# One ring of five buffers for the raw weights and their low part, four buffers for the high part, and a split that runs three units ahead

## What is computed

```python
c_act = jax.nn.silu(c)
for i in range(DEPTH):                                  # 2 layers
    mod = c_act @ ada_w[i] + ada_b[i]                   # 1024 x 6144 each
    sh1, sc1, g1, sh2, sc2, g2 = jnp.split(mod[:, None, :], 6, axis=-1)
    h = rms_norm(x, norm_mix[i]) * (1.0 + sc1) + sh1
    if i % N_MIXERS == 0:
        y = dilated_attention(h, attn_w_qkv[a], attn_w_out[a], ...)   # w_qkv 1024 x 9216
    else:
        y = hgrn2_mixer(h, hgrn_w_in[a], hgrn_w_out[a], ...)          # w_in 1024 x 4096
    x = x + g1 * y
    h = rms_norm(x, norm_ffn[i]) * (1.0 + sc2) + sh2
    x = x + g2 * (jax.nn.silu(h @ w1) * (h @ w3)) @ w2                # 1024 x 2816, twice, and 2816 x 1024
```

## Time and profile before

| | |
|---|---|
| runs of the kernel before | 910.11 us median of 3 (909.47 to 910.36) |
| the profiled execution | span 910.1 us from the first to the last instruction; no other time lies around it in the run times |
| busy in it | PE 847.7 us, DVE 623.6 us, ACT 426.3 us, POOL 119.3 us |
| granted clock of PE | 0.980 of full speed over the span |
| DMA | 188.96 MB, 208 GB/s over the span |

### The profile page before, as it was taken

One profiled execution on the slowest core, in us unless ns is written; L12 is line 12 of the kernel. 1 busy time (PEld: TensorE's weight loads), 2 busy tenths in 40 slices (PEclk: granted clock), 3 DMA queues, 4 the chain that ended last, 5 costly groups with the idle time before them and its releaser, 6 DMA issues.

```text
span 910.1 us, 10752 instructions
## 1 busy us (share of the span) xinstructions
PE 847.7 (93%) x4195; PEld 709.3 (78%) x4195; DVE 623.6 (69%) x749; ACT 426.3 (47%) x515; POOL 119.3 (13%) x159
## 2 busy tenths in 40 slices
PE   1599999999999979999999979999989799999997
PEld 0477888889888858888888857888877588888886
DVE  5879678677686767766777775895774754454543
ACT  3255446545455355333433446658554553433431
POOL 4101001010010010111111100462620000000000
PEclk9999999999999999999999979999979899999999
DMA  9899766876767627889889835444224175555541
GB/s 339 284 271 310 240 224 214 274 222 231 230 221 243 190 89 249 286 277 316 283 278 318 294 109 182 139 139 139 93 93 139 46 225 191 185 185 185 185 139 46
DMA packets 119607, 188.96 MB, mean 208 GB/s; under 512 B 5580, under 2 KB 90758, under 8 KB 119558
## 3 DMA queue, kind: packets, MB, share of 16 engines
q1 hardware_dynamic: 105350, 137.90, 47.4%
q0 software_dynamic: 14208, 50.39, 15.9%
HBM read 187.18 MB, written 1.09 MB: 207 GB/s over the span
## 4 chain that ended last, share of the span: by engine, by line
PE 81%; DVE 8%; DMA 4%; ACT 3%; issue 2%; SPq 2%; DVEq 0%; ACTq 0%
PE bank L390 69%; PE bank L659 2%; PE bank L508 2%; PE bank L484 2%; DMA raw<-in_attn_w_qkv_dram 1%; DVE wlo L1052 1%; PE bank L469 1%; PE bank L604 1%; ACT arena L774 1%; PE bank L434 1%; SPq L268 1%; PE bank L406 1%; DMA arena<-in_distance_table_dram 1%; DMA bias_rows<-arena 1%; DMA ada_w<-in_ada_w_dram 1%
## 5 line engine op out<-in xcount | busy, mean ns | idle before, releaser
L1052 DVE TENSOR_TENSOR wlo<-raw,whi 128x2048 fp32r<-128x2048 f32 x126 | 288.7, 2291 | 126.6 <-ACT whi L724 126.3
L390 PE MATMUL bank<-whi,hT_hi 128*128 128x512 f32 (+1 forms) x800 | 315.7, 395 | 8.7 <-DVE hT_lo L1145 8.3
L724 ACT ACTIVATE whi<-raw 128x2048 fp32r<-128x2048 f32 x126 | 241.5, 1916 | 150.3 <-PE bank L390 120.5
L390 PE MATMUL bank<-whi,hT_lo 128*128 128x512 f32 (+1 forms) x800 | 308.5, 386 | 0.0
L390 PE MATMUL bank<-wlo,hT_hi 128*128 128x512 f32 (+1 forms) x800 | 308.0, 385 | 0.0
L390 PEld LDWEIGHTS bank<-whi,hT_hi 128*128 128x128 f32 x800 | 152.7, 191 | 42.6 <-DVE hT_lo L1145 10.1
L390 PEld LDWEIGHTS bank<-whi,hT_lo 128*128 128x128 f32 x800 | 152.4, 191 | 30.4
L390 PEld LDWEIGHTS bank<-wlo,hT_hi 128*128 128x128 f32 x800 | 152.8, 191 | 28.8 <-issue 1.0
L1077 DVE SCALAR_TENSOR_TENSOR acc<-ada_w,cact,acc 128x1024 f32<-128x1024 f32 x80 | 102.3, 1279 | 25.0 <-DMA ada_w<-in_ada_w_dram 24.6
L390 PE MATMUL bank<-whi,oT_hi 128*128 128x512 f32 x240 | 97.4, 406 | 3.6 <-DVE oT_lo L1430 1.6
L312 POOL DMA_DIRECT2D ada_w<-in_ada_w_dram x80 | 42.6, 532 | 408.3 <-DVE acc L1077 408.3
(11 more groups left out here) (137 smaller groups left out, 734.0 us busy)
## 6 DMA issues: line engine op xcount, KB each, us to landing
raw<-in_ffn_w_dram SPq DMA_DIRECT2D x88, 512.0 KB, 4.9
ada_w<-in_ada_w_dram POOLq DMA_DIRECT2D x80, 512.0 KB, 5.2
raw<-in_attn_w_qkv_dram SPq DMA_DIRECT2D x64, 512.0 KB, 4.8
raw<-in_ffn_w_dram SPq DMA_DIRECT2D x22, 1024.0 KB, 6.0
raw<-in_hgrn_w_in_dram SPq DMA_DIRECT2D x16, 1024.0 KB, 5.4
arena<-in_ada_w_dram POOLq DMA_DIRECT2D x16, 512.0 KB, 6.6
raw<-in_attn_w_qkv_dram SPq DMA_DIRECT2D x4, 1024.0 KB, 5.1
raw<-in_attn_w_out_dram SPq DMA_DIRECT2D x4, 1024.0 KB, 6.0
```

Source lines behind the costliest of these rows:

```text
L390: mm = nc.tensor.matmul(d[:, 0:n], l, r[:, k, cut], start=first and k == 0 and q == 0, stop=last and k == nk - 1 and q == 2)
L724: return nc.scalar.activation(dst, src, ACT.Copy)
L1052: nc.vector.tensor_tensor(wlo[:, m % SPL, :], raw[:, m % RAW, :], fp(whi[:, m % SPL, :]), ALU.subtract).then_inc(s["split"], 1)
```

## The change

`raw` and `wlo` become two views of one piece of memory with five buffers. The split of unit `m` now writes `raw - whi` over the raw weights of the same buffer, so the buffer is free for the next load when PE is through with the unit, and not when DVE has split it: the load of unit `m` waits for PE's unit `m-5` (`pe_unit`). `whi` gets four buffers in place of three; the rounding of unit `m` waits for PE's unit `m-4`. `AHEAD` is 3: beside PE's unit `m` stands round and split of unit `m + 3`, and unit 2 is rounded and split in front of the loop. Together the buffers take nine units of memory, as before, and 64 bytes.

```diff
-RAW = 3
-SPL = 3
-AHEAD = 2
+RAW = 5
+SPL = 4
+AHEAD = 3
...
-        raw = sb("raw", [P, RAW, UNIT])
+        ring_at = -(-nc.sbuf_base // 64) * 64
+        ring = sb("ring", [P, RAW * UNIT + 16])
+        raw = nc.alloc_sbuf_tensor_at("raw", [P, RAW, UNIT], F32, offset=ring_at)
+        wlo = nc.alloc_sbuf_tensor_at("wlo", [P, RAW, UNIT], F32R, offset=ring_at)
         whi = sb("whi", [P, SPL, UNIT], F32R)
-        wlo = sb("wlo", [P, SPL, UNIT], F32R)
...
                 if m >= RAW:
-                    sp.wait_ge(s["split"], m - RAW + 1)
+                    sp.wait_ge(s["pe_unit"], m - RAW + 1)
...
-                sl = m % SPL
-                w = [v[:, sl, :].rearrange("p (k n) -> p k n", k=nk) for v in (whi, wlo)]
+                w = [v.rearrange("p (k n) -> p k n", k=nk) for v in (whi[:, m % SPL, :], wlo[:, m % RAW, :])]
...
             norm_round(0, 1)
+            round_unit(2)
...
-                nc.vector.tensor_tensor(wlo[:, m % SPL, :], raw[:, m % RAW, :], fp(whi[:, m % SPL, :]), ALU.subtract
+                nc.vector.tensor_tensor(wlo[:, m % RAW, :], raw[:, m % RAW, :], fp(whi[:, m % SPL, :]), ALU.subtract
...
             norm_rest(0, 1)
+            split_unit(2)
```

## The result

| | before | changed |
|---|---|---|
| median | 909.47 us (907.99 to 910.36, 5 runs) | 918.28 us (913.22 to 920.66, 5 runs) |
| ratio | | 1.0089, 95% interval 1.0063 to 1.0115 |
| profiled execution, span | 910.1 us | 918.9 us |
| granted clock | 0.980 | 0.978 |

A forecast was written before the change was run, and what follows sets the result against it. PE, busy 93% of the span, was taken to bound the kernel, with DVE on the path at the start. 910.1 + 3.8 (start) + 2.6 (clock) + 0 (later loads) = 916.5 us; range 911.9 to 921.

The forecast's parts named there:

- signs of being wrong: Wrong if load 3 moved, PE waited ahead of L604, or boundaries changed length; units from 10 on should last as before.
- What bounds the kernel, nothing to gain from the depth: Whole kernel: PE busy 93% of the span; its waits for split units, all a deeper split could save, are 0.2 us.
- The start, 3.8 us: Before the first block's transposes: reordered DVE work ends the first normalisation later, bounds 3.4 to 4.3 us, taken as 3.8.
- two feared waits: At the start, DVE waiting for load 4 before split 4, and for the third `ada_op`'s DMA: 0 to 0.8 us each.
- The clock, 2.6 us: Behind PE's gap of 5.7 us at the start: half clock costs dense matmuls 1.7 to 4.1 us, taken as 2.6.
- The later loads, 0 us: First network: ACT waits for most of some 29 loads, roughly 40 us in all, but PE loses 0.
- the cover: Slack before PE's transposes in the first network: landings up to 9.0 us tolerated, some 0.3 us spare at the worst.
- Equal size, equal time for the matmuls: Whole kernel: rounding, split and matmuls as many as before and of the same size, so no cost in the sum.
- rival "faster": Second boundary, behind unit 72: freer DMA engines win up to 2.7 us, giving 907.4; chance 0.07 together with a trace rule.

The follow-up runs named there:

- E8: Changed kernel without the 64 bytes behind the ring, `AHEAD` back at 2 and unit 2 not prepared ahead of the loop: 908.18 us, 0.9996 of before.
- E7: Changed kernel without the 64 bytes, and with round and split behind the other work in the first three steps: 909.10 us, 1.0005 of before.
- E5: Changed kernel without the 64 bytes behind the ring: 914.05 us, 1.0065 of before.
- E3: Changed kernel with round and split behind the other work in the first three steps, 64 bytes kept: 914.00 us, 1.0059 of before.
- E4: Changed kernel with 20 matmuls of 512 columns put into PE's gap behind unit 3: 917.69 us, 1.0092 of before.
- E11: E5 with 20 matmuls put into PE's gap behind unit 3: 914.37 us, 1.0059 of before.
- E12: E7 with each load waiting for one more unit of PE, m-4 instead of m-5: 1019.66 us, 1.1219 of before.
- E6: Kernel before with 64 unused bytes between `whi` and `wlo`, nothing else: 922.58 us, 1.0160 of before.
- E9: Kernel before with the first block squared and normalised earlier and the first network's `ada_op` spread over 30 steps: 907.35 us, 0.9982 of before.
- E1: Kernel before with 64 unused bytes behind the raw ring: 908.32 us, 1.0003 of before.
- E2: Changed kernel with 128 instead of 64 unused bytes behind the ring: 921.45 us, 1.0142 of before.
- E10: E5 with the first block squared and normalised earlier and the first network's `ada_op` spread over 30 steps: 908.37 us, 0.9997 of before.

## Why the prediction was right

The number was right, and so was the mechanism of its two terms, the order at the start and the clock behind the gap. But the sum of the two was 6.4 us and 8.8 were measured; the missing part is the balance of things that the prediction had at nothing, and that they nearly cancelled is luck. Three of its own signs of being wrong came: load 3 is split 0.3 us later, the boundaries change length, and the units from 10 on are not as long as before.

*What bounds the kernel, nothing to gain from the depth.* Right, and shown by E8 and E7: neither ring nor depth moves the time by what can be measured.

*The start, 3.8 us.* The row of DVE's work is the one predicted, 13.3 us from split 3 to the end of the normalisation, where 13.28 had been added up. Neither of the two feared waits came: split 4 started when DVE was free, and the third `ada_op` too. PE's transposes begin 3.7 us later (72.99 against 69.28): 3.4 of gap, and 0.3 because load 3, taken as fixed, came later (split 3 at 59.62 against 59.34), which is more chance than cause, since E5 with the same order has it at 59.05. E3 shows the cause: the old order takes the gap from 5.26 to 0.84 us. In the medians, E5 against E7, which differ by this order alone, it is 914.05 against 909.10 us; that holds gap and clock, 5.0 us, where the sum had 6.4. Their profiles say the same: a gap of 5.30 against 1.82 us, and 3.4 us at half clock, worth 1.7.

*The clock, 2.6 us.* In the trace 2.7 us (+3.71 at the transposes, +6.46 at unit 5), and 2.7 us from E4; in E5, with the same gap, only 1.7. The forecast lies between the two, and which of them an execution has was not predicted. That a busy PE takes the half clock away is shown twice, E4 and E11. That the kernel's time falls by it is not: other half-clock stretches of 3.4 us and more come and go from profile to profile. One of the five runs of the changed kernel took 913.22 us at a clock of 0.985, the others 917.82 to 920.66 at 0.978 to 0.981.

*The later loads, 0 us.* ACT waits 34 us for loads in the first network, forecast some 40, but in 11 places and not at most of 29 loads: the landings took 3.8/5.0/8.0 us there, where 4.6/6.6/8.7 had been carried over from before. The transposes were never late in the profiled execution. Two things were missed. Unit 72, the last of the first network, stands directly behind the low part it needs, and PE waits 0.8 us for it (1.0 to 2.0 in E3, E4, E5 and E7): the cover was worked out for the eleven places ahead of the transposes and not for this one. And the cover is as thin as said: in E11's profile PE waits 1.78 us ahead of one set of transposes, and E12 shows what lies behind it.

*Equal size, equal time for the matmuls.* This step failed. It was stated in one clause ("of the same size") and priced at nothing. The 64 spare bytes behind the ring move `whi` out of its distance to `wlo` and slow every matmul a little: 4.9 us between E3 and E7 (914.00 and 909.10), which differ by this alone. The sum came out near the truth since another term, the boundary, ran the other way: 2.0 us won in the changed kernel and about 3 in E5 and E7 (from the end of unit 72 to unit 73: 10.6 us before, 8.6, 7.3 and 7.5). The rival "faster" had seen the place: before, DVE ends its last `ada_op` 0.1 us ahead of PE, in the changed kernel 2.1 us ahead. In the changed kernel this is no speed of DVE's: PE comes later, slowed by the 64 bytes and its wait, and E6, the old kernel with slow matmuls, has 8.4 us there too. The ring is not needed for it: E9 gets to 7.3 us by the order of DVE's work alone. Nor is the depth: E8 has 8.2 with `AHEAD = 2`.

So 8.8 us in the profiled pair are 3.7 of a later start of the transposes, 2.7 of clock, and 2.3 as the balance of slower matmuls, the wait ahead of unit 72 and shorter boundaries. The cause of the loss, order and padding, is shown by E7, in which nothing is left of it.

## What to carry to other kernels

A deeper buffer is worth what the consumer waited for it, here 0.2 us; read that before asking what it could bring. It is not free though: it moves prefetch work ahead of other work in the queues of the engines that prepare it, and at the start of the kernel, where these engines are already behind, each such operation goes straight into the time. A load that waits for the consumer in place of the preparing engine loses its lead, and since the waiting rounding stands in one queue with the work that is due now, depth does not make up for it. When buffers are laid out anew, keep the distances of the operands to each other, and compare the time of a fixed row of matmuls before and after.

## What was not expected of the hardware

Where the operands of PE lie to each other changes the rate of matmuls of 128x512, though E6 has every instruction of before. With `whi` and `wlo` a multiple of 8192 bytes apart 72 of them take 16.35 us, in the eight kernels of this kind whose second network shows such a row (before, E1, E5, E7 to E11). With the ring and 64 bytes beyond such a multiple it is 16.52, with 128 bytes 16.64; in the kernel before, with fixed pairs of buffers, 64 bytes make 16.87. Why, and why the fixed pairs suffer more, stays open, and so does whether the distance to the third operand has a part in it; only 0, 64 and 128 bytes beyond a multiple were tried.

The low clock also comes in dense stretches. In the profiles of E2, E4, E5, E6, E7, E9 and E11, but not in those of before, the change, E1, E3, E8 and E10, 3.4 us near 230 to 240 us were granted at half speed, beginning between 0.3 us ahead of the end of sixteen one-column matmuls (L434, L435 in some kernels) and 1.4 us behind it. The other six have the same sixteen matmuls and no such stretch, so these alone do not bring it, and nothing that was tried explains which profiles have it. E12 is left out here, since its PE waits in many more places.
